# The last pair's sums and stores started earlier, and two gate products moved forward, in a hybrid encoder layer on one core

## The chip, the cores and the metric

The kernel runs on one core of one Trainium2 chip. Its time is the device time of one execution in microseconds (us). Three executions of the kernel before took 1149.3, 1150.73 and 1148.74 us; their median is 1149.3 us.

## The reference, cut to what matters

The layer is applied to two sequences of 512 tokens (prompt and sample) with the same weights, all in fp32, width 1024, feed-forward width 2816. Only the feed-forward part is touched:

```python
up = _dwconv3(_rmsnorm(x, norm2) @ w_up, conv_w, conv_b)     # (512, 5632), three taps along the tokens
gate, val = up[..., :D_FF], up[..., D_FF:]
x = x + (jax.nn.silu(gate) * val) @ w_down                   # (512, 2816) @ (2816, 1024)
g = jax.nn.sigmoid(_rmsnorm(x, norm3) @ w_ple_gate + b_ple_gate)
x = x + (p @ w_ple_proj) * g
```

## The kernel before, in words

Every matrix product is done in two parts: an operand is split into a high part (rounded, written by ScalarE) and a low part (the difference, written by VectorE), and TensorE adds three products, high by high, low by high, high by low (`mm3`, L297 to L299). So each tile that TensorE reads must have passed ScalarE first and VectorE second. The semaphores `w_hi`, `g_hi`, `uw_hi` count the high parts, `w_lo`, `g_lo`, `uw_lo` the low parts.

**The up projection** runs over 22 feature tiles, taken as 11 pairs (NPAIR = 11, `last` = 10), each pair in two blocks f = 0 and f = 1. A block is seven products over sums and differences of quarters of the operands (the kinds "1", "6", "5", "2", "7", "3", "4" of `STEADY`, in that order), 12 matmuls each. Three of them share accumulator banks that VectorE combines in between: `add_u2` (L2108), `add_v` (L2114) and `add_c22` (L2121). TensorE's kind "7" waits for `add_v`, kind "4" for `add_c22`. VectorE also splits the weights (`up_lo`, L2032), adds the outer taps (L2131, L2139) and multiplies silu(gate) by val (`product`, L2146; it counts `g_ready`). ScalarE does the centre tap, silu and the high parts. GpSimd forms the weight sums (`combine`, L2514). Pair 0 has an own entry part; pair 1 is the first one in steady order, and its VectorE block (1, 0) also holds the two products that are left over from pair 0's second block (`behind`).

**For the down projection** the kernel needs, of each pair, sums of the gated values (four tiles S, `sum_s`, L2553) and of `w_down` (four tiles T, `sum_t`, L2558). GpSimd makes both in SBUF (SB and TB, in XT) and SyncE's DMA queue stores them to HBM (`store_s` L516, `store_t` L526). They are laid down in HBM since all pairs are read back later: the down projection is 77 units n = 0 to 76, seven passes p over the 11 pairs k, and each unit needs one 256 KB weight tile (`load_down`, L579) and one 256 KB tile of activations (`load_g`, L586 or L588). There are four buffers for each; ScalarE splits (L1575, L1583), VectorE splits (L2229, L2233), TensorE does 12 matmuls. Pass 0 reads neither S nor T. Pass 1 (from unit 11) reads T tile 3 and S tile 1 of each pair, its last unit, 21, those of the last pair. When the sums are stored, their place in XT takes the residual back from HBM (`load_x2`, L537).

**What sets the order.** Each engine runs its own list in the order written, and blocks on the semaphore waits in front of an instruction. SyncE's list is one queue: a wait in it holds up every transfer behind it. `load_down(n)` waits for `w_lo` of unit n - 4, `load_g(n)` for `g_lo` of unit n - 4. GpSimd's list for the last pair is s_late and t_sums of pair 9, then a wait `g_lo >= 8` (L2620, low parts of units 0 to 7), then `s_early`, `s_pair`, `s_late` and `t_sums` of pair 10: eight operations in 128x512 fp32. `s_early` needs `g_ready` 42, `s_pair` needs 44, which is the last product of the up projection.

Of the kernel before, what the change touches and what calls it, by code (L numbers as in the profile page):

```python
# [38 lines left out]
NPAIR = FT // 2  # L39
# [47 lines left out]
def encoder(nc, x, p_in, w, y, consts):  # L87
    with ExitStack() as ctx:
# [3 lines left out]
        def sem(name):  # L92
            return ctx.enter_context(nc.semaphore(name))
# [61 lines left out]
        def quarter(f, r):  # L155

            return RAW[f][:, r // 2, 4 * (r % 2):4 * (r % 2) + 4, :]

        def s1_buf(f):
            return (RB[:, :], R[:, 1, :])[f].rearrange("p (k m) -> p k m", k=4)  # L160
# [23 lines left out]
        def up_w(v, k):  # L184

            return v[:, 1 - k // 2, 4 * (k % 2):4 * (k % 2) + 4, :]
# [44 lines left out]
        s_sum, s_out, t_in, t_sum, t_out = (sem(n) for n in ("s_sum", "s_out", "t_in", "t_sum", "t_out"))  # L231
# [33 lines left out]
        g_hi, g_lo, dn_tile, dn_ready, dn_free = (sem(n) for n in ("g_hi", "g_lo", "dn_tile", "dn_ready", "dn_free"))  # L265
# [132 lines left out]
        def _(sp):  # L398
# [108 lines left out]
            def store_g(i, f):  # L507
                sp.wait_ge(g_ready, i * 4 + (2 * f + 2))
                if f:
                    sp.dma_start(g_dram[:, 1:3, bass.ds(i * S, S)], SG[:, 1]).then_inc(g_out[1], 16)  # L510
                else:
                    sp.dma_start(g_dram[:, 0, bass.ds(i * S, S)], SG[:, 0, 1]).then_inc(g_out[0], 16)

            def store_s(i):
                sp.wait_ge(s_sum, i * 4 + 4)
                sp.dma_start(s_dram[:, bass.ds(i * 4 * S, 4 * S)], XT[:, 0:4 * S]).then_inc(s_out, 16)  # L516
# [7 lines left out]
            def store_t(i):  # L524
                sp.wait_ge(t_sum, i * 4 + 4)
                sp.dma_start(t_dram[:, bass.ds(i * 4 * S, 4 * S)], TB).then_inc(t_out, 16)  # L526
# [9 lines left out]
            def load_x2(q):  # L536
                sp.dma_start(XT[:, q * 2048:(q + 1) * 2048], xt_dram[:, q * 2048:(q + 1) * 2048]).then_inc(xt_back[q], 16)  # L537
# [32 lines left out]
            def load_down(n):  # L570
                p, k = divmod(n, NPAIR)
                if n >= 4:
                    sp.wait_ge(w_lo, T_DN + n - 3)
                if DN_W[p] is None:
                    tile = t_dram[:, (4 * k + DN_T[p]) * S:(4 * k + DN_T[p] + 1) * S]
                else:
                    f, h = DN_W[p]
                    tile = w["w_down"][(2 * k + f) * P:(2 * k + f + 1) * P, h * S:(h + 1) * S]
                sp.dma_start(up_w(WR, d_slot(n)), tile.rearrange("p (a m) -> p a m", m=P)).then_inc(wd_in[n % 4], 16)  # L579

            def load_g(n):
                p, k = divmod(n, NPAIR)
                if n >= 4:
                    sp.wait_ge(g_lo, n - 3)
                if DN_G[p] is None:
                    sp.dma_start(AR[:, n % 4, :], s_dram[:, (4 * k + DN_S[p]) * S:(4 * k + DN_S[p] + 1) * S]).then_inc(g_in[n % 4], 16)  # L586
                else:
                    sp.dma_start(AR[:, n % 4, :], g_dram[:, DN_G[p], k * S:(k + 1) * S]).then_inc(g_in[n % 4], 16)  # L588

            last = NPAIR - 1  # L590
# [11 lines left out]
            for n in range(4, NU):  # L602
                if n == last:
                    sp.wait_ge(g_out[0], 16 * NPAIR)
                if n == NPAIR:
                    sp.wait_ge(t_out, 16 * last)
                    sp.wait_ge(s_out, 16 * last)
                if n == 16:
                    sp.wait_ge(t_out, 16 * NPAIR)
                    load_x2(1)  # L610
                if n == 17:
                    sp.wait_ge(s_out, 16 * NPAIR)
                    load_x2(0)
                if n == 2 * NPAIR:
                    sp.wait_ge(g_out[1], 16 * NPAIR)
                load_down(n)
                load_g(n)
                if n == 4:
                    store_g(last, 1)
                if n == 12:  # L620
                    store_s(last)
                if n == 14:
                    store_t(last)
                if n == 8:
                    sp.wait_ge(conv_done, 4 * FT)
                    sp.wait_ge(pt_out, 16)
                    sp.dma_start(SF[:, 2048:4096], pt_dram).then_inc(p_in_sem, 16)

            def store(s):
                for t in range(TT):  # L630
                    g = s * TT + t
                    sp.wait_ge(f_out, 2 * (g + 1))
                    sp.dma_start(y[s][t * P:(t + 1) * P, :], OT[:, g % 3, :]).then_inc(out_done[g % 3], 16)
# [1063 lines left out]
        def _(dve):  # L1697
            def f32(v):
                return v.bitcast(F32)
# [329 lines left out]
            def up_lo(raw, k_slot, count):  # L2029

                dve.wait_ge(uw_hi, count)
                dve.tensor_tensor(up_w(WL, k_slot), raw, f32(up_w(WH, k_slot)), ALU.subtract).then_inc(uw_lo, 1)  # L2032
# [71 lines left out]
            def add_u2(i, f, steady=True):  # L2104

                dve.wait_ge(m_done, done_at("6", i, f, steady))
                dve.wait_ge(m_copied, copy_at(0, i, f, steady))
                dve.tensor_tensor(ps[4 * f + 1][:, :], ps[4 * f + 1][:, :], E1[:, f, :], ALU.add).then_inc(m_summed, 1 if steady else 2)  # L2108

            def add_v(i, f, steady=True):  # L2110

                dve.wait_ge(m_copied, copy_at(1, i, f, steady))
                dve.wait_ge(m_summed, sum_at(0, i, f, steady))
                dve.tensor_tensor(ps[4 * f + 2][:, :], ps[4 * f + 1][:, :], M5C[:, f, :], ALU.add).then_inc(m_summed, 1 if steady else 2)  # L2114

            def add_c22(i, f, steady=True):

                dve.wait_ge(m_done, done_at("7", i, f, steady))
                if steady:
                    dve.wait_ge(conv_done, i * 8 + (4 * f - 6))  # L2120
                dve.tensor_tensor(ps[4 * f + 3][:, :], ps[4 * f + 1][:, :], M5C[:, f, :], ALU.add).then_inc(m_summed, 1 if steady else 2)  # L2121
# [20 lines left out]
            def product(i, f, s):  # L2142

                dve.wait_ge(silu_done, i * 4 + (2 * f + s + 1))
                dve.wait_ge(conv_done, i * 8 + (4 * f + (4, 2)[s]))
                dve.tensor_tensor(SG[:, f, s, :], SG[:, f, s, :], CV[:, s, :], ALU.mult).then_inc(g_ready, 1)  # L2146
# [38 lines left out]
            def up_block(i, f, more=True, behind=False):  # L2185

                base = 7 * f
                up_lo(quarter(f, 2), UP_SLOT["7"], i * 14 + (base + 5))
                add_u2(i, f)
                if not behind:  # L2190
                    up_lo(quarter(f, 1), UP_SLOT["3"], i * 14 + (base + 6))
                add_v(i, f)
                if behind:
                    up_lo(quarter(f, 1), UP_SLOT["3"], i * 14 + (base + 6))
                up_lo(quarter(f, 3), UP_SLOT["4"], i * 14 + (base + 7))
                if more:
                    up_lo(quarter(1 - f, 1), UP_SLOT["2"], i * 14 + (base + 8))
                add_c22(i, f)
                if behind:
                    product(0, 1, 1)  # L2200
                    product(0, 1, 0)
                tap_left(i, f, 0)
                if more:
                    up_lo(quarter(1 - f, 0), UP_SLOT["1"], i * 14 + (base + 9))
                tap_right(i, f, 0)
                tap_left(i, f, 1)
                if more:
                    up_lo(S2, UP_SLOT["6"], i * 14 + (base + 10))
                tap_right(i, f, 1)
                tap_left(i, f, 2)  # L2210
                if more:
                    up_lo(s1_buf(1 - f), UP_SLOT["5"], i * 14 + (base + 11))
                tap_right(i, f, 2)
                tap_left(i, f, 3)
                product(i, f, 1)
                tap_right(i, f, 3)
                product(i, f, 0)
# [6 lines left out]
            last = NPAIR - 1  # L2224
# [158 lines left out]
        def _(pool):  # L2383
# [88 lines left out]
            for i in range(HEADS // 2):  # L2472
                last = i == HEADS // 2 - 1
# [87 lines left out]
            def s_early(i):  # L2561

                pool.wait_ge(s_out, i * 16)
                pool.wait_ge(g_ready, i * 4 + 2)
                sum_s(SB[:, 2, :], SG[:, 0, 1, :], SG[:, 0, 0, :], ALU.subtract, i * 4 + 1)
# [51 lines left out]
            up_sums(NPAIR - 1, 1)  # L2617
            s_late(NPAIR - 2)
            t_sums(NPAIR - 2)
            pool.wait_ge(g_lo, 8)  # L2620
            s_early(NPAIR - 1)
            s_pair(NPAIR - 1)
            s_late(NPAIR - 1)
# [60 lines left out]
```

## Time and profile before

| | |
|---|---|
| profiled execution, time | 1149.3 us |
| its span (first to last instruction) | 1147.5 us |
| median of three runs | 1149.3 us |
| TensorE busy | 1116.6 us, 97% |
| VectorE busy | 820.4 us, 71% |
| ScalarE busy | 559.3 us, 49% |
| GpSimd busy | 464.8 us, 41% |
| DMA, mean over the span | 141 GB/s |

The table is read with the engines in mind: TensorE is hardly ever idle, so only idle time of TensorE, and what ends it, can change the time. The profiled execution's time lies 1.8 us above its span, and equals the median, so a change of the span is read as the same change of the median.

### The profile page before, as it was taken

What the parts mean: (1) busy time and instruction counts of PE and PEld (TensorE: products, weight loads), DVE (VectorE), ACT (ScalarE), POOL (GpSimd) and SP (SyncE); (2) the same over time, 40 slices, a digit from 0 to 9 for tenths busy, and PEclk for the clock granted to TensorE, in tenths of its full rate; (3) what the DMA queues carried; (4) which work ended last, traced back from release to release, by engine and by line L of the source; (5) the groups of instructions that cost most, each with busy time, mean ns of one, the idle gap of its engine ahead of it and who ended that gap; (6) DMA issues with size and microseconds to landing.
All of it is one profiled execution on the core that took longest, in us unless ns stands there. A gap on an engine that the chain in (4) does not pass through costs nothing.

```text
span 1147.5 us, 15785 instructions
## 1 busy us (share of the span) xinstructions
PE 1116.6 (97%) x5120; PEld 894.5 (78%) x5120; DVE 820.4 (71%) x1164; ACT 559.3 (49%) x992; POOL 464.8 (41%) x405
## 2 busy tenths in 40 slices
PE   7999999999999989999999999999999999999996
PEld 6788766665888867888888888888888888888885
DVE  6594876773458799878787878787876757757565
ACT  6412577775223454445454545454564546544332
POOL 0176542322567046856585558556210202201000
PEclk9999999999999999999999999999999999999999
DMA  6611000104653116443644364435896565534341
GB/s 208 215 32 44 1 12 12 38 6 148 214 202 120 55 41 223 158 162 121 210 144 157 119 210 153 149 128 182 334 340 207 187 201 191 174 105 121 92 142 74
DMA packets 138432, 161.61 MB, mean 141 GB/s; under 512 B 8755, under 2 KB 105354, under 8 KB 133770
## 3 DMA queue, kind: packets, MB, share of 16 engines
q1 hardware_dynamic: 138080, 160.82, 41.9%
q8 instruction: 29, 0.48, 0.2%
q14 instruction: 25, 0.20, 0.1%
q10 hardware_dynamic: 298, 0.11, 0.0%
HBM read 115.55 MB, written 45.35 MB: 140 GB/s over the span
## 4 chain that ended last, share of the span: by engine, by line
PE 85%; DVE 9%; ACT 2%; issue 2%; POOL 1%; ACTq 0%; DVEq 0%; POOLq 0%
PE ps L297 26%; PE ps L299 26%; PE ps L298 26%; PE ps L859 2%; PE ps L840 2%; DVE WL L2032 1%; PE ps L710 1%; ACT SF L1173 1%; PE ps L851 1%; DVE SF L2131 1%; DVE SF L2139 1%; DVE WDHL L1889 1%; DVE col L1900 1%; PE ps L671 0%; DVE R L1882 0%
## 5 line engine op out<-in xcount | busy, mean ns | idle before, releaser
L297 PE MATMUL ps<-XH,WH 128*128 128x512 f32 x722 | 287.9, 399 | 2.0 <-DVE WL L2032 0.8
L299 PE MATMUL ps<-XH,WL 128*128 128x512 f32 x722 | 281.5, 390 | 0.0
L298 PE MATMUL ps<-XL,WH 128*128 128x512 f32 x722 | 281.4, 390 | 0.0
L297 PEld LDWEIGHTS ps<-XH,WH 128*128 128x128 f32 x722 | 135.9, 188 | 34.4 <-issue 5.4
L298 PEld LDWEIGHTS ps<-XL,WH 128*128 128x128 f32 x722 | 135.9, 188 | 29.2 <-issue 2.2
L299 PEld LDWEIGHTS ps<-XH,WL 128*128 128x128 f32 x722 | 135.7, 188 | 28.5
L297 PE MATMUL ps<-GHL,WH 128*128 128x512 f32 x394 | 153.5, 390 | 1.4 <-DVE WL L2032 1.4
L298 PE MATMUL ps<-GHL,WH 128*128 128x512 f32 x394 | 153.3, 389 | 0.0
L299 PE MATMUL ps<-GHL,WL 128*128 128x512 f32 x394 | 153.3, 389 | 0.0
L333 ACT ACTIVATE WH<-WR 128x1024 fp32r<-128x1024 f32 (+3 forms) x45 | 45.5, 1011 | 137.8 <-PE ps L299 124.1
L1466 ACT ACTIVATE SF<-ps,col 128x512 f32<-128x512 f32 x88 | 68.3, 779 | 74.5 <-PE ps L299 65.5
L2229 DVE TENSOR_TENSOR WL<-WR,WH 128x512 fp32r<-128x512 f32 x77 | 58.2, 756 | 59.8 <-ACT WH L1575 59.8
L1575 ACT ACTIVATE WH<-WR 128x512 fp32r<-128x512 f32 x77 | 48.6, 632 | 93.0 <-PE ps L299 74.0
L2633 POOL TENSOR_TENSOR SF<-SF 128x512 f32<-128x512 f32 x16 | 24.1, 1504 | 168.0 <-ACT SF L1618 168.0
L297 PEld LDWEIGHTS ps<-GHL,WH 128*128 128x128 f32 x394 | 74.0, 188 | 17.4 <-issue 2.1
L299 PEld LDWEIGHTS ps<-GHL,WL 128*128 128x128 f32 x394 | 74.0, 188 | 15.3
L298 PEld LDWEIGHTS ps<-GHL,WH 128*128 128x128 f32 x394 | 74.0, 188 | 15.3
L338 DVE TENSOR_TENSOR WL<-WR,WH 128x1024 fp32r<-128x1024 f32 (+3 forms) x45 | 61.5, 1366 | 24.7 <-ACT WH L333 24.2
L2558 POOL TENSOR_TENSOR XT<-XT 128x512 f32<-128x512 f32 x44 | 68.8, 1563 | 11.8 <-DMA XT<-in_w_down 7.7
L2139 DVE SCALAR_TENSOR_TENSOR SF<-ps,col,SF 128x511 f32<-128x511 f32 x88 | 65.2, 741 | 0.4
L2131 DVE SCALAR_TENSOR_TENSOR SF<-ps,col,SF 128x511 f32<-128x511 f32 x88 | 64.8, 737 | 0.0
L2032 DVE TENSOR_TENSOR WL<-TL,WH 128x512 fp32r<-128x512 f32 x54 | 50.4, 933 | 18.6 <-ACT WH L1422 18.6
(237 smaller groups left out, 2245.6 us busy)
## 6 DMA issues: line engine op xcount, KB each, us to landing
TL<-in_w_up SPq DMA_DIRECT2D x48, 256.0 KB, 3.6
s_scratch<-XT SPq DMA_DIRECT2D x11, 1024.0 KB, 4.7
XT<-in_w_down SPq DMA_DIRECT2D x11, 1024.0 KB, 6.5
t_scratch<-XT SPq DMA_DIRECT2D x11, 1024.0 KB, 3.8
WR<-t_scratch SPq DMA_DIRECT2D x44, 256.0 KB, 2.7
TL<-s_scratch SPq DMA_DIRECT2D x44, 256.0 KB, 2.9
WR<-in_w_up SPq DMA_DIRECT2D x40, 256.0 KB, 3.3
WR<-in_w_down SPq DMA_DIRECT2D x33, 256.0 KB, 4.1
```

What stands on the lines that cost most here:

```text
L297: pe.matmul(out, wh, xh, start=first, stop=False, skip_group_check=skip)
L298: pe.matmul(out, wh, xl, start=False, stop=False, skip_group_check=skip)
L299: return pe.matmul(out, wl, xh, start=False, stop=last, skip_group_check=skip)
L333: act.activation(WH[:, slot(n), base:cols, :], WR[:, slot(n), base:cols, :], ACT.Copy).then_inc(w_hi, 1)
L338: dve.tensor_tensor(WL[:, slot(n), base:cols, :], WR[:, slot(n), base:cols, :], WH[:, slot(n), base:cols, :].bitcast(F32), ALU.subtract).t ...
L1466: act.activation(out, ps[4 * f + bank][:, :], ACT.Identity, scale=taps_of(1, val, f), bias=taps_of(3, val, f)).then_inc(tap1, 1)
L1575: act.activation(up_w(WH, d_slot(n)), up_w(WR, d_slot(n)), ACT.Copy).then_inc(w_hi, 1)
L2032: dve.tensor_tensor(up_w(WL, k_slot), raw, f32(up_w(WH, k_slot)), ALU.subtract).then_inc(uw_lo, 1)
L2131: dve.scalar_tensor_tensor(out[:, 1:S], ps[4 * f + bank][:, 0:S - 1], taps_of(0, val, f), out[:, 1:S], ALU.mult, ALU.add).then_inc(tap0, 1)
L2139: dve.scalar_tensor_tensor(out[:, 0:S - 1], ps[4 * f + bank][:, 1:S], taps_of(2, val, f), out[:, 0:S - 1], ALU.mult, ALU.add).then_inc(con ...
L2229: dve.tensor_tensor(up_w(WL, d_slot(n)), up_w(WR, d_slot(n)), f32(up_w(WH, d_slot(n))), ALU.subtract).then_inc(w_lo, 1)
L2558: pool.tensor_tensor(out, a, b, ALU.subtract).then_inc(t_sum, 1)
```

## The change

1. VectorE, block (1, 0): the two products left over from pair 0 come before the low parts of kind "4"'s and the next block's weights, no longer behind `add_c22`.
2. GpSimd: the wait `g_lo >= 8` before the last pair's `s_early` goes.
3. SyncE: the last pair's S store goes behind the loads of unit 6 (before: unit 12), its T store behind unit 9 (before: 14). Before the loads of unit 11 the queue waits until both stores have landed (before: those of pair 9). The two loads of the residual are issued behind the loads of units 11 and 14, with no wait of their own (before: ahead of units 16 and 17, after waits for the two stores).

```diff
                 if n == NPAIR:
-                    sp.wait_ge(t_out, 16 * last)
-                    sp.wait_ge(s_out, 16 * last)
-                if n == 16:
                     sp.wait_ge(t_out, 16 * NPAIR)
-                    load_x2(1)
-                if n == 17:
                     sp.wait_ge(s_out, 16 * NPAIR)
-                    load_x2(0)
...
                 load_down(n)
                 load_g(n)
...
-                if n == 12:
+                if n == 6:
                     store_s(last)
-                if n == 14:
+                if n == 9:
                     store_t(last)
...
+                if n in (NPAIR, NPAIR + 3):
+                    load_x2(1 if n == NPAIR else 0)
...
                 if behind:
                     up_lo(quarter(f, 1), UP_SLOT["3"], i * 14 + (base + 6))
+                    product(0, 1, 1)
+                    product(0, 1, 0)
                 up_lo(quarter(f, 3), UP_SLOT["4"], i * 14 + (base + 7))
                 if more:
                     up_lo(quarter(1 - f, 1), UP_SLOT["2"], i * 14 + (base + 8))
                 add_c22(i, f)
-                if behind:
-                    product(0, 1, 1)
-                    product(0, 1, 0)
...
             t_sums(NPAIR - 2)
-            pool.wait_ge(g_lo, 8)
             s_early(NPAIR - 1)
```

VectorE in block (1, 0), before: from `add_v` (out ps2) over the two weight parts of kinds "3" and "4" (WR), that of the next block (TL), `add_c22` (out ps3) and the two products to the first tap.

```order
L2114 TENSOR_TENSOR ps2<-ps1,SF 128x512 [waits m_summed,m_copied]
L2032 TENSOR_TENSOR WL<-WR,WH 128x512 [waits uw_hi] x2
L2032 TENSOR_TENSOR WL<-TL,WH 128x512 [waits uw_hi]
L2121 TENSOR_TENSOR ps3<-ps1,SF 128x512 [waits conv_done,m_done]
L2146 TENSOR_TENSOR SF<-SF 128x512 [waits conv_done,silu_done] x2
L2131 SCALAR_TENSOR_TENSOR SF<-ps0,col,SF 128x511 [waits tap1]
```

The same stretch of VectorE in the changed kernel, whose lines are numbered 4 lower here.

```order
L2110 TENSOR_TENSOR ps2<-ps1,SF 128x512 [waits m_summed,m_copied]
L2028 TENSOR_TENSOR WL<-WR,WH 128x512 [waits uw_hi]
L2142 TENSOR_TENSOR SF<-SF 128x512 [waits conv_done,silu_done] x2
L2028 TENSOR_TENSOR WL<-WR,WH 128x512 [waits uw_hi]
L2028 TENSOR_TENSOR WL<-TL,WH 128x512 [waits uw_hi]
L2117 TENSOR_TENSOR ps3<-ps1,SF 128x512 [waits conv_done,m_done]
L2127 SCALAR_TENSOR_TENSOR SF<-ps0,col,SF 128x511 [waits tap1]
```

The products moved ahead of two weight parts and of `add_c22`; nothing is added or removed.

SyncE before, from the loads of unit 6 to those of unit 11: no store stands between them (SF<-pt_scratch is the transfer behind unit 8).

```order
L588 DMA TL<-g_scratch 128x512 [waits g_lo]
L579 DMA WR<-in_w_down 128x512 [waits w_lo]
L588 DMA TL<-g_scratch 128x512 [waits g_lo]
L579 DMA WR<-in_w_down 128x512 [waits w_lo]
L588 DMA TL<-g_scratch 128x512 [waits g_lo]
L627 DMA SF<-pt_scratch 128x2048 [waits pt_out,conv_done]
L579 DMA WR<-in_w_down 128x512 [waits w_lo]
L588 DMA TL<-g_scratch 128x512 [waits g_lo]
L579 DMA WR<-in_w_down 128x512 [waits w_lo,g_out0]
L588 DMA TL<-g_scratch 128x512 [waits g_lo]
L579 DMA WR<-t_scratch 128x512 [waits w_lo,s_out,t_out]
```

SyncE in the changed kernel, from the S store behind unit 6 to the first residual load behind unit 11.

```order
L516 DMA s_scratch<-XT 128x2048 [waits s_sum]
L579 DMA WR<-in_w_down 128x512 [waits w_lo]
L588 DMA TL<-g_scratch 128x512 [waits g_lo]
L579 DMA WR<-in_w_down 128x512 [waits w_lo]
L588 DMA TL<-g_scratch 128x512 [waits g_lo]
L621 DMA SF<-pt_scratch 128x2048 [waits pt_out,conv_done]
L579 DMA WR<-in_w_down 128x512 [waits w_lo]
L588 DMA TL<-g_scratch 128x512 [waits g_lo]
L526 DMA t_scratch<-XT 128x2048 [waits t_sum]
L579 DMA WR<-in_w_down 128x512 [waits w_lo,g_out0]
L588 DMA TL<-g_scratch 128x512 [waits g_lo]
L579 DMA WR<-t_scratch 128x512 [waits w_lo,s_out,t_out]
```

Two 1 MB stores with a wait each now stand among the loads of units 7 to 10, and the wait ahead of unit 11 is for these stores.

## Rows read from the trace of the kernel before

**Rows 1.** Busy time from 457 to 1100 us; columns are named in the first line.
```profile
core 0: us, PE busy (x) PEld busy (x) DVE busy (x) ACT busy (x) POOL busy (x), PEclk, DMA share, GB/s
457.00:1100.00 643.00, 643.00 (x2850) 532.04 (x2849) 471.10 (x651) 311.09 (x517) 265.73 (x183) 1.00 0.52 175
```
**Rows 2.** TensorE's waits from 405 to 1100 us, all of them.
```profile
PE ps L297 <- DVE WL L2032: 4.4, 4, 2.2
PE ps L297 <- DVE ps L2114: 1.1, 2, 0.6
```
**Rows 3.** Timeline of DVE, block (1, 0): start, duration, instruction.
```profile
436.57 2.38 DVE L2032 TENSOR_TENSOR WL<-WR,WH 128x512 fp32r<-128x512 f32 x2
438.88 1.77 DVE L2032 TENSOR_TENSOR WL<-TL,WH 128x512 fp32r<-128x512 f32 x1
440.57 0.69 DVE L2121 TENSOR_TENSOR ps<-ps,SF 128x512 f32<-128x512 f32 x1
441.18 1.28 DVE L2146 TENSOR_TENSOR SF<-SF 128x512 f32<-128x512 f32 x2
...
455.88 0.68 DVE L2114 TENSOR_TENSOR ps<-ps,SF 128x512 f32<-128x512 f32 x1
```
**Rows 4.** Timeline of POOL in the same stretch.
```profile
436.64 1.77 POOL L2514 TENSOR_TENSOR R<-R,TL 128x512 f32<-128x512 f32 x1
...
442.60 1.29 POOL L2553 TENSOR_TENSOR XT<-XT,SF 128x512 f32<-128x512 f32 x1 [2.50 <-DVE SF L2146]
```
**Rows 5.** Timeline of PE: start of kind "4", then start of the next kind "7".
```profile
442.31 0.39 PE L297 MATMUL ps<-CHL,WH 128*128 128x512 f32 x1
...
456.62 0.50 PE L297 MATMUL ps<-WDHL,WH 128*128 128x512 f32 x1 [0.55 <-DVE ps L2114]
456.96 0.40 PE L298 MATMUL ps<-WDHL,WH 128*128 128x512 f32 x1
```
**Rows 6.** Timeline of DVE: last product, low parts of unit 3; then units 9 and 11.
```profile
812.92 0.69 DVE L2146 TENSOR_TENSOR SF<-SF 128x512 f32<-128x512 f32 x1
813.53 0.69 DVE L2229 TENSOR_TENSOR WL<-WR,WH 128x512 fp32r<-128x512 f32 x1
814.13 0.69 DVE L2233 TENSOR_TENSOR GHL<-TL,GHL 128x512 fp32r<-128x512 f32 x1
...
828.51 1.75 DVE L2233 TENSOR_TENSOR GHL<-TL,GHL 128x512 fp32r<-128x512 f32 x1
...
835.30 1.78 DVE L2233 TENSOR_TENSOR GHL<-TL,GHL 128x512 fp32r<-128x512 f32 x1
```
**Rows 7.** Timeline of POOL: sums of pair 9, then of the last pair.
```profile
794.65 6.19 POOL L2558 TENSOR_TENSOR XT<-XT 128x512 f32<-128x512 f32 x4 [7.72 <-DMA XT<-in_w_down]
823.11 3.36 POOL L2553 TENSOR_TENSOR XT<-SF 128x512 f32<-128x512 f32 x2 [22.26 <-DVE GHL L2233]
```
**Rows 8.** Timeline of PE: first matmuls of units 0, 6 and 17.
```profile
807.63 0.39 PE L297 MATMUL ps<-GHL,WH 128*128 128x512 f32 x1
...
823.96 0.39 PE L297 MATMUL ps<-GHL,WH 128*128 128x512 f32 x1
...
853.94 0.47 PE L297 MATMUL ps<-GHL,WH 128*128 128x512 f32 x1
```
**Rows 9.** Timeline of SyncE's queue: unit 13, the T store, the first residual load.
```profile
830.14 0.43 SPq L579 DMA_DIRECT2D WR<-t_scratch  x1
...
836.56 0.34 SPq L526 DMA_DIRECT2D t_scratch<-XT  x1
...
841.43 0.33 SPq L537 DMA_DIRECT2D XT<-xt_scratch  x1
```
**Rows 10.** Timeline of ACT: high parts of units 6 (activations) and 13 (weights).
```profile
820.33 0.63 ACT L1583 ACTIVATE GHL<-TL 128x512 fp32r<-128x512 f32 x1
...
835.33 0.63 ACT L1575 ACTIVATE WH<-WR 128x512 fp32r<-128x512 f32 x1 [0.76 <-DMA WR<-t_scratch]
```
**Rows 11.** DMA from 816 to 828 us, mean rate of all transfers.
```profile
DMA packets 2107, 4.64 MB, mean 387 GB/s; under 512 B 233, under 2 KB 233, under 8 KB 1978
```

## The prediction

> **What bounds the kernel now.** I read the busy shares first: TensorE is busy 1116.6 of 1147.5 us. Next the busy time by stretch: from 457 to 1100 us TensorE's busy time fills the whole 643.00 us [rows 1]. Then its waits: from 405 to 1100 us there are six in all, 5.5 us, all on VectorE [rows 2], and all of them before 457. The down projection, where the larger part of the change lies, has nothing to give back; it can only lose, by a wait that is new there. So I asked how much lead VectorE and the DMAs have over TensorE, and what the earlier GpSimd work does to it. For that I read the timelines of the two places side by side.
>
> **How GpSimd costs VectorE time.** A low part takes VectorE 0.69 us alone (unit 3 [rows 6]). While GpSimd runs sums, the same instructions last 1.75 to 1.78 us, and from 828.51 to 835.30 four starts lie (835.30 - 828.51) / 4 = 1.70 us apart [rows 6], against 0.60 us (813.53 to 814.13). In that stretch GpSimd's sums follow each other at the same step. The two engines take turns, each waiting until the other's operation is over, and one GpSimd operation costs VectorE 1.10 us. Operations of VectorE that read an accumulator bank keep their time (`add_c22`, 0.69 us [rows 3]).
>
> **Part 1, the two products in block (1, 0).** Before, behind `add_v`: two weight parts, 436.57 to 438.95, with a GpSimd operation (436.64 [rows 4]) between them; the third from 438.88 to 440.65, also held up by GpSimd; `add_c22` at 440.57, the products at 441.18, alone: 1.28 us for both [rows 3]. TensorE starts kind "4" at 442.31 with no wait [rows 5], 1.05 us after `add_c22` is done (441.26).
> Now: the products take the second and third place, so they are what the same two GpSimd operations hold up, and end at 440.65. They release GpSimd's `s_pair_copied`, which came 0.14 us after the products before (442.46 to 442.60 [rows 3, 4]), so it is ready at 440.79. VectorE's second weight part starts at 440.57 and goes first, GpSimd is next, and the third weight part, issued at 441.17, takes the long form, 1.77 us, to 442.94. `add_c22` starts at 442.86 and ends at 443.55, TensorE's kind "4" at 443.60 (0.05 us of passing on: `add_v` ends at 456.56, kind "7" starts at 456.62 [rows 3, 5]). That is a new wait of 443.60 - 442.31 = 1.29 us. A start after a wait costs 0.11 us more, as 456.62 to 456.96 is 0.34 us where the usual step is 0.23 [rows 5]. New loss: 1.40 us.
> What goes in return: kind "7" would start at 442.31 + 5 x 2.72 = 455.91 and started at 456.62 [rows 5], a loss of 0.71 + 0.11 = 0.82 us. In the new order TensorE gets there at 457.31, and VectorE's chain, with the same work, at about 456.5, so this wait goes. Net: 1.40 - 0.82 = +0.58 us. Bounds: -0.8 (the old wait goes and the new one doesn't come, if GpSimd's sums don't get between) and +1.4.
>
> **Part 2, the removed wait on GpSimd.** Pair 9's sums end at 794.65 + 6.19 = 800.84 [rows 7]; `s_early` can follow at once, in a time when VectorE has little to do. `s_pair` needs the last product, done at 812.92 + 0.69 = 813.61 [rows 6]. So seven operations (two, one, four) start about 813.75 in place of 823 to 836. The load for the T sums stands in SyncE's queue where it stood, ahead of unit 4's tiles, so it is no obstacle. VectorE then has units 3 to 6 to split. The low weight part of unit 3 is already running (813.53), and from 814.13 on each of the next seven low parts takes a turn with one GpSimd operation:
> activations of unit 3 from 814.13 to 815.91; of unit 4 from 817.53 to 819.31; of unit 5 from 820.93 to 822.71; of unit 6 from 824.33 to 826.11 (step 2 x 1.70, duration 1.78).
> TensorE's units start at 807.63 + 2.72 n (unit 6: 823.96 [rows 8]), so they would start at 815.79, 818.51, 821.23 and 823.96. Its lags are 0.17, 0.85, 1.53 and 826.16 - 823.96 = 2.20 us, with the slow start 2.31 us. The high parts are no limit (unit 6's is done at 820.96 [rows 10]). Then GpSimd is done (814.2 + 7 x 1.70 = 826), and VectorE does a unit in 1.2 us against TensorE's 2.72. Before, the same contention fell on units 8 to 11 with some 4 us of lead, and was hidden. Bounds: 0 if VectorE keeps a lead I don't see, and 7 x 1.10 - 0.97 = 6.7 us if none of it is absorbed beyond unit 3's lead (814.82 to 815.79). I take 2.3, since it is a count of turns at a pitch that rows show.
> Unit 17 started 0.06 us late, and slow, at 853.94 [rows 8], behind the residual loads; these come earlier now, so I take off 0.1 us.
>
> **Part 3, SyncE's queue.** The S store waits for `s_late`, the third operation, at about 818.9, and unit 7's loads stand behind it. The T store goes at about 825.7, and unit 11's loads wait until it has landed. The busy queue moves 387 GB/s [rows 11], 2.7 us per 1 MB; a T store with nothing ahead of it took 841.43 - 836.56 = 4.9 us [rows 9], so a transfer starts some 2.2 us after its issue. Unit 13's tile, issued at 830.14 right behind an S store, was taken up at 835.33 [rows 9, 10], 5.2 us later. So unit 7's tiles are there by 825.0, and split behind unit 6 by 827.3, against 826.67 + 2.3 = 829.0. The T store here queues behind seven transfers and lands about 832.8 instead of 830.5. Unit 11's tiles land at 836.1, are split by 837.5, and are needed at 837.55 + 2.3 = 839.9. Unit 12, behind a residual load of 1 MB, lands at 840.0, split 841.4, needed 842.6. The thinnest margin is 1.2 us, so I take 0; at 10% less rate unit 12 would lose some 0.5 us. The bounds are 0 and 4 us (worked out with the rivals).
> The page on DMA in the Trainium skill ("DMA: Bandwidth & Descriptors", section Bandwidth) puts the limit of traffic between HBM and SBUF at about 358 GB/s per core, below the 387 that this trace shows for 12 us. By an estimate from that page each megabyte takes 2.9 us, unit 12's tiles come about 1.4 us later, and the sum would be higher by about 0.3 us; the trace's rate is used.
>
> **The sum.** 0.58 + 2.31 - 0.1 + 0 = +2.8 us, on the profiled execution's span 1147.5 and on its time 1149.3, which is the median: 1152.1 us. Nothing behind takes it back, since TensorE has no other wait until 1100 us [rows 1].
>
> **The rivals.**
> *The contention is absorbed.* GpSimd's turns fall where VectorE would idle, as they did for units 8 to 11. Part 1 alone is left: 1149.9 us. For it: two low parts alone take 1.2 us of a unit's 2.72, so VectorE has slack on average. Against it: with turns they take 3.4 us, and the lead of 0.97 us at unit 3 is smaller than one turn of 1.70. Chance 0.18.
> *SyncE's stops decide.* The wait for the T store ahead of unit 11 and 4.5 MB of early transfers leave the tiles of units 10 to 12 late. At 310 GB/s (1 MB in 3.4 us) unit 10's tiles are ready at 839.5, needed at 837.1, and unit 12 adds 1.8: +4.1 more, 1156.2 us. It decides once the T store lands behind about 835. For it: the DMAs are saturated there. Against it: the rate of rows 11. Chance 0.14.
> *Not slower: VectorE's block (1, 0) really gets shorter.* The products go early enough that GpSimd's first sum of S is behind the third weight part; `add_c22` is then at 441.8, kind "4" waits for nothing and the 0.82 us at 456 go, and in the down projection the turns leave VectorE the precedence. The time would be 1149.3 - 0.8 = 1148.5 us. It decides if GpSimd needs over 0.4 us from the products to its sum; the row says 0.14. Chance 0.08.
> *The change does nothing in its larger part*, if GpSimd's sums were held by something else until 823. The only wait of theirs that fell so late is that on VectorE's low part of activations [rows 7], so I give this nothing of its own.
>
> **Chances and range.** Forecast 0.60, with its own range 1151.2 to 1153.6; absorbed 0.18; stops 0.14; shorter 0.08. Two tenths of a per cent, 2.3 us, is about what a measurement of this kernel can tell from no change. Of the forecast's own case I put 0.46 above +2.3 us and 0.14 below. Slower: 0.46 + 0.14 = 0.60. Faster by that much isn't reachable by any mechanism here: 0.03 for the unseen. Same: 0.37. The range for 8 in 10 is 1149.5 to 1155.5 us: it takes in the absorbed case and half way to the stops.
>
> **What would show it.** Part 1: a wait of TensorE of some 1.3 us on `add_c22` about 442, and none on `add_v` about 456. Part 2: GpSimd's seven sums from 813.7 to about 826, low parts of 1.7 us there, and four waits of TensorE on the low parts of units 3 to 6, growing to 2.2 us in total. Part 3: no wait of TensorE on DMA-fed parts of units 7 to 12. I am wrong if the low parts stay at 0.69 us beside GpSimd's sums, if units 3 to 6 start on time, or if units 10 to 12 start late.

## The result, and the profile after

The changed kernel takes 1158.3 us (median of four, 1157.69 to 1158.83) against 1150.0 us in the same runs: a ratio of 1.0067, 95% interval 1.0052 to 1.0082, so +6 to +9 us. The forecast was +2.8 us, with 1155.5 as the upper end. It is slower, as forecast, but by about 8 us. Of ten executions of the changed kernel on record nine took 1156.8 to 1158.9 us and one 1154.5.

The profiled execution took 1158.92 us, its span is 1157.1 (before: 1149.3 and 1147.5), so 9.6 us are to be found. TensorE's waits, all of them from 400 to 1100 us, are the first view (engine, tile and line, what it waited for: us, times, longest). To them belong the two rows of before [rows 2].

```profile
PE ps L297 <- DVE GHL L2228: 5.0, 5, 3.5
PE ps L297 <- DVE WL L2028: 4.4, 4, 2.1
PE ps L297 <- DVE ps L2117: 1.2, 1, 1.2
PE ps L297 <- DVE ps L2110: 0.5, 1, 0.5
```

Where these waits are shows in TensorE's timeline: kind "4" of block (1, 0), then units 4, 5, 6, 10 and 12, each with the wait in brackets.

```profile
444.58 0.50 PE L297 MATMUL ps<-CHL,WH 128*128 128x512 f32 x1 [1.17 <-DVE ps L2117]
...
821.01 0.47 PE L297 MATMUL ps<-GHL,WH 128*128 128x512 f32 x1 [0.42 <-DVE GHL L2228]
824.41 0.47 PE L297 MATMUL ps<-GHL,WH 128*128 128x512 f32 x1 [0.43 <-DVE GHL L2228]
827.79 0.47 PE L297 MATMUL ps<-GHL,WH 128*128 128x512 f32 x1 [0.40 <-DVE GHL L2228]
...
839.14 0.47 PE L297 MATMUL ps<-GHL,WH 128*128 128x512 f32 x1 [0.22 <-DVE GHL L2228]
848.38 0.47 PE L297 MATMUL ps<-GHL,WH 128*128 128x512 f32 x1 [3.55 <-DVE GHL L2228]
```

A wait in brackets is about 0.17 us less than the start moved by, since a matmul is drawn 0.39 us long and the next one starts 0.23 us after it. So I account by starts:

| stretch | how it is read | us |
|---|---|---|
| to `add_v` of block (1, 0), before anything changed | 436.93 - 435.97 | +0.96 |
| to unit 0 | 809.20 - 807.63, less the 0.96 | +0.61 |
| units 0 to 6 | 827.79 - 809.20 = 18.59, before 16.33 [rows 8] | +2.26 |
| units 6 to 12 | 848.38 - 840.27 = 8.11 late, less 3.83 | +4.28 |
| unit 12 to the last unit | 1027.1 - 848.38 = 178.72, before 1017.5 - 840.27 = 177.23 | +1.49 |

The sum is 9.60 us; the tail adds nothing. The first entry lies ahead of every changed instruction, so it is not the change's; that it is there is one reason why this pair of profiles shows more than the medians do.

VectorE and GpSimd in block (1, 0) (compare [rows 3, 4]; everything is 0.96 us later here):

```profile
437.54 0.68 DVE L2028 TENSOR_TENSOR WL<-WR,WH 128x512 fp32r<-128x512 f32 x1
438.13 3.48 DVE L2142 TENSOR_TENSOR SF<-SF 128x512 f32<-128x512 f32 x2
441.54 0.68 DVE L2028 TENSOR_TENSOR WL<-WR,WH 128x512 fp32r<-128x512 f32 x1
442.14 1.78 DVE L2028 TENSOR_TENSOR WL<-TL,WH 128x512 fp32r<-128x512 f32 x1
443.85 0.68 DVE L2117 TENSOR_TENSOR ps<-ps,SF 128x512 f32<-128x512 f32 x1
```

```profile
441.76 1.61 POOL L2548 TENSOR_TENSOR XT<-XT,SF 128x512 f32<-128x512 f32 x1 [0.69 <-DVE SF L2142]
```

The two products last 3.48 us instead of 1.28, the third weight part is held up by GpSimd's sum, and `add_c22` stands at 443.85.

The same two engines in the down projection (compare [rows 6, 7]): low parts of units 3, 4 and 6, and GpSimd's first and last sums.

```profile
815.69 1.79 DVE L2228 TENSOR_TENSOR GHL<-TL,GHL 128x512 fp32r<-128x512 f32 x1
817.40 1.77 DVE L2224 TENSOR_TENSOR WL<-WR,WH 128x512 fp32r<-128x512 f32 x1
...
825.88 1.77 DVE L2228 TENSOR_TENSOR GHL<-TL,GHL 128x512 fp32r<-128x512 f32 x1
```

```profile
815.32 1.61 POOL L2548 TENSOR_TENSOR XT<-SF 128x512 f32<-128x512 f32 x1 [11.52 <-DVE SF L2142]
...
820.39 6.71 POOL L2553 TENSOR_TENSOR XT<-XT 128x512 f32<-128x512 f32 x4
```

Seven sums, seven long low parts. Up to here it is as predicted. What wasn't is in SyncE's queue: the S store, the T store, unit 11's weights behind the wait, the residual load, unit 12's activations (compare [rows 9]). Below them stands ScalarE taking up unit 11's activations, then unit 12's weights and activations.

```profile
820.34 0.34 SPq L516 DMA_DIRECT2D s_scratch<-XT  x1
...
827.13 0.34 SPq L526 DMA_DIRECT2D t_scratch<-XT  x1
...
836.39 0.33 SPq L579 DMA_DIRECT2D WR<-t_scratch  x1
...
837.24 0.43 SPq L537 DMA_DIRECT2D XT<-xt_scratch  x1
...
838.20 0.42 SPq L586 DMA_DIRECT2D TL<-s_scratch  x1
```

```profile
839.75 0.63 ACT L1579 ACTIVATE GHL<-TL 128x512 fp32r<-128x512 f32 x1
845.62 0.63 ACT L1571 ACTIVATE WH<-WR 128x512 fp32r<-128x512 f32 x1 [5.24 <-DMA WR<-t_scratch]
846.88 0.63 ACT L1579 ACTIVATE GHL<-TL 128x512 fp32r<-128x512 f32 x1 [0.63 <-DMA TL<-s_scratch]
```

The queue stands still from 828.45 to 836.39 us. Unit 11's tiles, the first behind the stop, are there 3.4 us after it ends (839.75). Unit 12's activations, issued at 838.20, are there only 8.7 us later. Between the two is the residual's megabyte, issued at 837.24 and landed 7.7 us later, at 844.9 (last figure of the line, from issue to landing):

```profile
XT<-xt_scratch SPq DMA_DIRECT2D x1, 1024.0 KB, 7.7
```

So it landed 5.2 us after unit 11's tiles, and unit 12's tiles landed behind it. The busy time by stretch shows DMA and clock (last three columns: granted clock, DMA share, GB/s):

```profile
836.00:838.00 2.00, 2.00 (x10) 1.65 (x10) 0.30 (x1) 0.97 (x2) 0.00 (x0) 1.00 0.34 77
838.00:840.00 2.00, 1.78 (x9) 1.18 (x8) 1.27 (x3) 1.16 (x3) 0.00 (x0) 1.00 0.86 300
...
849.50:853.50 4.00, 4.00 (x13) 3.10 (x12) 3.55 (x6) 4.00 (x10) 0.00 (x0) 0.57 0.98 371
853.50:856.00 2.50, 2.50 (x13) 2.05 (x12) 1.84 (x4) 2.40 (x6) 0.00 (x0) 1.00 0.79 262
```

The DMAs nearly run dry (77 GB/s) before unit 11's and 12's tiles and the 1 MB come at once. And TensorE's granted clock falls behind the wait: 0.57 over 4 us, 13 matmuls where 17.6 fit at a step of 0.227 us. So time was lost here while TensorE was busy, which the statement ahead of the prediction, that only idle time of TensorE can change the time, leaves out.

### The profile page after: what moved, and what is told of

Same layout as the page of the kernel before. It is cut to its first block, busy times and chain, and to the rows that moved or that the text cites. A ratio compares the mean times of both kernels' runs of the same rounds, so it can differ in the third digit from the quotient of the medians.

```text
span 1157.1 us, 15784 instructions
## 1 busy us (share of the span) xinstructions
PE 1120.7 (97%) x5120; PEld 896.1 (77%) x5120; DVE 822.5 (71%) x1164; ACT 558.3 (48%) x992; POOL 465.3 (40%) x405
## 4 chain that ended last, share of the span: by engine, by line
PE 83%; DVE 8%; DMA 2%; issue 2%; ACT 2%; POOL 2%; SPq 0%; DVEq 0%; POOLq 0%; ACTq 0%
PE ps L297 25%; PE ps L299 25%; PE ps L298 25%; PE ps L855 2%; PE ps L836 2%; DVE WL L2028 1%; DMA t_scratch<-XT 1%; PE ps L706 1%; DMA TL<-s_scratch 1%; ACT SF L1169 1%; PE ps L847 1%; DVE SF L2127 1%; DMA SF<-in_x_prompt 1%; DVE WDHL L1885 1%; PE ps L667 1%
```

## The experiments

Ratios are against the kernel before, run beside each kernel; the us behind them are differences of medians, by the intervals good to about 1 us each way. A table of all profiles stands at the end of this section. Theory A is that three separate costs add up: turns in block (1, 0), turns at units 3 to 6, and SyncE's stop together with the residual load ahead of unit 12.

**e1, the products alone.** The change's part 1 on the kernel before.

```diff
                 if behind:
                     up_lo(quarter(f, 1), UP_SLOT["3"], i * 14 + (base + 6))
+                    product(0, 1, 1)
+                    product(0, 1, 0)
...
                 add_c22(i, f)
-                if behind:
-                    product(0, 1, 1)
-                    product(0, 1, 0)
```

> The kernel before with the two products moved alone. Theory A (what was predicted, and what the profile after seems to show): a wait of TensorE of about 1.2 us on add_c22 at kind 4 of block (1, 0), none on add_v at the next kind 7, +0.6 us in all (1150.6 against 1150.0), no other wait behind. Theory B (the whole loss is SyncE's queue in the down projection and the products cost nothing): +0.0 us, no wait on add_c22.

Measured: 1151.4 against 1150.7 us, ratio 1.0008 (0.9999 to 1.0017), +0.7 us. In the trace the wait is on `add_c22`, that on the next `add_v` is gone:

```profile
PE ps L297 <- DVE ps L2121: 1.2, 1, 1.2
PE ps L297 <- DVE GHL L2232: 0.6, 1, 0.6
PE ps L297 <- DVE ps L2114: 0.5, 1, 0.5
PE ps L297 <- issue: 0.4, 1, 0.4
```

A's mechanism is confirmed; its +0.6 us lies within the interval, but so does zero. Not expected: waits at unit 17 (0.58) and unit 11 (0.35), where nothing was changed.

**e2, GpSimd's wait alone removed**, on the kernel before.

```diff
             t_sums(NPAIR - 2)
-            pool.wait_ge(g_lo, 8)
             s_early(NPAIR - 1)
```

> The kernel before with GpSimd's wait removed alone; SyncE's queue as before. Theory A: GpSimd's seven sums from about 813.7 to 826 us, VectorE's low parts there 1.7 to 1.8 us each, TensorE late at units 4, 5 and 6 (about 0.4 us each, growing to 2.3 us), none at unit 10 or 12, granted clock 1.00 throughout: +2.3 us. Theory B (the waits of units 4 to 6 come from late tiles, and go with the old queue): units 3 to 6 on time, +0.0 us.

Measured: 1151.5 us, ratio 1.0007 (0.9997 to 1.0016), +0.8 us. The trace has the waits of 0.42, 0.43 and 0.40 us at units 4, 5, 6 (821.02, 824.42, 827.82) with the old queue, so they don't come from late tiles: B falls. But A's total of +2.3 us, a ratio of 1.0020, lies outside the interval, and zero inside; the profiles of e9 and the table below say why.

**e3, the changed kernel with the old SyncE queue.** Stores, waits and residual loads are back at their old places.

```diff
-                if n == 6:
+                if n == 12:
                     store_s(last)
-                if n == 9:
+                if n == 14:
                     store_t(last)
...
-                if n in (NPAIR, NPAIR + 3):
-                    load_x2(1 if n == NPAIR else 0)
```

> The changed kernel with SyncE's queue as it was before: both other parts stay. Theory A: the sum of the two, +2.9 us; the waits of units 10 and 12 (0.2 and 3.6 us) and the fall of the granted clock behind unit 12 are gone, so 5.4 us less than the changed kernel. Theory B: as the kernel before, +0.0 us. Theory C (GpSimd's earlier sums also make the loads late, whatever the queue's order): a wait at unit 10 to 12 stays, +5 us or more.

Measured: 1153.3 us, ratio 1.0016 (1.0005 to 1.0027), +2.6 us. No wait at units 10 and 12, clock 1.00 from 846 to 856 us. So the queue's new order is worth about 1158.3 - 1153.3 = 5 us (different runs; 5.8 by the profiles), as A said, and C falls.

**e5, the stores early, the waits for them and the residual loads late.** On the changed kernel:

```diff
                 if n == NPAIR:
+                    sp.wait_ge(t_out, 16 * last)
+                    sp.wait_ge(s_out, 16 * last)
+                if n == 16:
                     sp.wait_ge(t_out, 16 * NPAIR)
+                    load_x2(1)
+                if n == 17:
                     sp.wait_ge(s_out, 16 * NPAIR)
+                    load_x2(0)
...
-                if n in (NPAIR, NPAIR + 3):
-                    load_x2(1 if n == NPAIR else 0)
```

> The changed kernel, with the stores at their new places (behind units 6 and 9), but the waits for them and the residual loads back where they were before (ahead of units 16 and 17). Theory A (unit 12 is late because the queue stands still until the T store has landed and a 1 MB residual load is ahead of its tiles): no wait at unit 12, the 0.2 us at unit 10 stays, +3.3 us against the kernel before. Theory D (the early stores alone, by their 2 MB among the loads of units 7 to 10, make units 10 to 12 late): the wait at unit 12 stays over 1 us, +5 us or more.

Measured: 1153.8 us, ratio 1.0025 (1.0014 to 1.0037), +3.1 us; only the three waits at units 4 to 6 in the down projection. The 2 MB of early stores by themselves cost no wait that the profile lists, not even the one at unit 10. D falls.

**e4, the stop stays, the residual loads late.** On the changed kernel:

```diff
+                if n == 16:
+                    load_x2(1)
+                if n == 17:
+                    load_x2(0)
...
-                if n in (NPAIR, NPAIR + 3):
-                    load_x2(1 if n == NPAIR else 0)
```

> The changed kernel with the wait for both stores still ahead of unit 11's loads, but the two residual loads back ahead of units 16 and 17. Theory A (unit 12 needs both: the stopped queue and the 1 MB ahead of its tiles): unit 11 as in the changed kernel, unit 12's tiles issued at about 837.3 us land by 842, no wait there or under 0.3 us, granted clock 1.00, +3.3 us against the kernel before, as with no hold. Theory E (the stop alone makes the queue late): a wait of 2 us or more at unit 12 stays, +5 us or more.

Measured: 1152.9 against 1151.5 us, ratio 1.0013 (1.0003 to 1.0022), +1.4 us. The stop is as long as in the changed kernel (T store issued at 824.30, unit 11's loads at 834.03), yet unit 12 is on time; unit 10 waits 0.63 us (the second line):

```profile
824.97 0.47 PE L297 MATMUL ps<-GHL,WH 128*128 128x512 f32 x1 [0.40 <-DVE GHL L2230]
...
836.78 0.47 PE L297 MATMUL ps<-GHL,WH 128*128 128x512 f32 x1 [0.63 <-DVE GHL L2230]
```

E falls. The smaller total than e5's is not a gain: this profile has the same waits as e5's and the one at unit 10 besides, and takes 0.8 us more from block (1, 0) on (table). The stop alone leaves unit 12 on time; the residual loads can't be had early without the stop, since they overwrite what the stores read, so that half wasn't tried alone.

**e6, the first residual load one unit later**, behind unit 12's loads.

```diff
-                if n in (NPAIR, NPAIR + 3):
-                    load_x2(1 if n == NPAIR else 0)
+                if n in (NPAIR + 1, NPAIR + 3):
+                    load_x2(1 if n == NPAIR + 1 else 0)
```

> The changed kernel with the first residual load one unit later, behind the loads of unit 12, the second behind unit 14 as before it. Theory A: unit 12 on time, unit 13 behind the 1 MB and late in its place, by 1 to 2 us since one unit more of lead was won; the granted clock falls behind it only if that wait is long enough, so this shows a wait between 0.4 us (clock kept in the units 4 to 6) and 3.55 us (clock lost). +4 to +6 us against the kernel before. Theory F (the residual load is slow in itself wherever it stands): a wait of 3.5 us as in the changed kernel, moved to unit 13.

Measured: 1154.7 us, ratio 1.0028 (1.0019 to 1.0037), +3.2 us. Unit 12 is on time, unit 13 waits, but 0.34 us, less than the 1 to 2 expected:

```profile
847.34 0.47 PE L297 MATMUL ps<-GHL,WH 128*128 128x512 f32 x1 [0.34 <-DVE GHL L2228]
```

The clock stays at 1.00 behind it. One place in the queue turns 3.55 us of waiting into 0.34, so F falls. Two things changed at once: unit 13 is needed 2.72 us after unit 12, and the megabyte itself came faster, 6.7 us from issue to landing where the changed kernel's took 7.7:

```profile
XT<-xt_scratch SPq DMA_DIRECT2D x1, 1024.0 KB, 6.7
```

**e7, memsets in place of the seven sums**, on the kernel before, with the old queue. This kernel leaves out seven of the last pair's eight sums. Its one execution took 1147.3 us.

```diff
-            pool.wait_ge(g_lo, 8)
             s_early(NPAIR - 1)
-            s_pair(NPAIR - 1)
-            s_late(NPAIR - 1)
-            t_sums(NPAIR - 1)
...
+            for j, q in enumerate((0, 1, 3)):
+                pool.memset(SB[:, q, :], 0.0).then_inc(s_sum, 1)
...
+            for j, q in enumerate((0, 1, 3, 2)):
+                pool.memset(TB[:, q, :], 0.0).then_inc(t_sum, 1)
```

> The kernel before without GpSimd's wait, and with the last pair's seven sums after s_early replaced by writes of zeros to the same tiles (this leaves out the last pair's sums). Theory A (two operations that read SBUF take turns): VectorE's low parts of units 3 to 6 at 0.69 us although GpSimd works at the same time, units 4 to 6 on time. Theory G (any GpSimd work or its semaphores there slow VectorE): low parts over 1 us and waits at units 4 to 6 as with the sums, though shorter.

The low parts beside GpSimd's memsets keep their 0.69 us, and no unit waits:

```profile
812.34 0.69 DVE L2233 TENSOR_TENSOR GHL<-TL,GHL 128x512 fp32r<-128x512 f32 x1
813.74 0.69 DVE L2229 TENSOR_TENSOR WL<-WR,WH 128x512 fp32r<-128x512 f32 x1 [0.71 <-ACT WH L1575]
814.37 0.69 DVE L2233 TENSOR_TENSOR GHL<-TL,GHL 128x512 fp32r<-128x512 f32 x1
```

```profile
811.95 1.70 POOL L2624 MEMSET XT<- 128x512 f32 x3 [11.53 <-DVE SF L2146]
813.70 2.28 POOL L2628 MEMSET XT<- 128x512 f32 x4
```

So it is not that GpSimd works, writes or signals there, but that its sums also read SBUF: G falls. The Trainium skill ("SBUF — State Buffer", section Who interferes with whom) says that a VectorE instruction with two SBUF inputs contends with a GpSimd one that reads SBUF, not with one that only writes. The trace agrees on both sides: 1.7 us per turn beside sums, 0.69 us beside memsets.

**e9 and e10, both kernels again.**

> The kernel before once more, for a second profile. Theory A: block (1, 0) and (1, 1) as before (waits of 0.5 us each on add_v), and waits of 0.3 to 0.6 us at unit 11 or 17 in this execution or not, since the leads there were 0.5 and 0 us in the first profile. Theory H: all units on time.

> The changed kernel once more, for a second profile. Theory A: waits of about 0.4 us at units 4, 5 and 6 and of 3 to 4 us at unit 12, with the granted clock down behind it. Theory I (the wait at unit 12 was an accident of one execution): under 1 us there.

The kernel before, in its second profile (1150.87 us), waits at units 11 and 17:

```profile
838.67 0.47 PE L297 MATMUL ps<-GHL,WH 128*128 128x512 f32 x1 [0.36 <-issue]
855.54 0.47 PE L297 MATMUL ps<-GHL,WH 128*128 128x512 f32 x1 [0.26 <-DVE GHL L2233]
```

H falls. Unit 11 starts 0.9 us late here (838.67 against 807.85 + 11 x 2.72 = 837.77), at the end of the sums' turns. The first profile (1149.3 us, the second fastest of four) happened to have only a trace of the second wait. Neither is in the profiles of e2, e3 and e5, where GpSimd's sums are early and TensorE runs 2.4 us later: e2 pays 2.4 us, and gets back 1.4 against an execution like this one. The changed kernel repeats itself: 0.39, 0.40, 0.40, then 0.35 at unit 10 and 3.43 at unit 12 (1159.21 us), and clock 0.58 from 849.5 to 853.5. I falls.

**e8, a version from the findings**, on the kernel before: three leads are widened.

```diff
-            pool.wait_ge(g_lo, 8)
             s_early(NPAIR - 1)
+            pool.wait_ge(g_lo, 8)
...
-                if n == 17:
+                if n == 20:
                     sp.wait_ge(s_out, 16 * NPAIR)
                     load_x2(0)
```

In block (1, 1), `add_v` also goes ahead of the low part of kind "3".

> A version made from the findings, on the kernel before: GpSimd's wait stands behind s_early, so that one of eight sums leaves the contended stretch; the second residual load goes ahead of unit 20 in place of 17; in block (1, 1) add_v comes before the low part of kind 3. Theory A: the wait on add_v at about 457 shrinks from 0.55 to about 0.1 us, no waits at units 11 and 17, which the kernel before shows in some executions (0.35 and 0.58 us in the run with the products alone): -0.6 us where those waits don't occur and -1.7 us where they do, so 1149 to 1150 against 1150.7. Theory H (these leads don't matter): +0.0 us.

Measured: 1149.0 against 1151.5 us, ratio 0.9977 (0.9966 to 0.9988), -2.6 us: faster than both kernels, by more than expected. The wait on `add_v` at 455 us fell to 0.18, and no unit waits. The profile accounts for 0.5 us against the first profile of the kernel before and 1.9 against the second (table); the rest of the 2.6 it doesn't show.

**e11 and e12, two of its three parts alone**: the hunk at `n == 17` of e8's diff, and the hunk at `g_lo`.

> Of the combined version only its second residual load: the kernel before, with it ahead of unit 20 instead of 17. Theory A (unit 17's tiles are late because two 1 MB loads stand ahead of them): no wait at unit 17, the 0.4 us at unit 11 may stay; -0.3 to -0.7 us. Theory J (the wait goes to unit 20 with the load): a wait there, +0.0 us.

> Of the combined version only the place of GpSimd's wait: the kernel before, with the wait behind s_early, so that seven sums and not eight fall among the units 8 to 11. Theory A (unit 11's 0.4 us wait is the end of that contention): no wait at unit 11; unit 17 may still be late by 0.1 to 0.7 us; -0.5 us. Theory K (unit 11's wait has nothing to do with the sums): it stays, +0.0 us.

The residual load at 20: 1150.2 us, ratio 1.0001 (0.9993 to 1.001), nothing measurable; its profile has no wait at unit 17 or 20, but the first profile of the kernel before has none that is listed either. GpSimd's wait moved: 1149.0 against 1150.6, ratio 0.9989 (0.9979 to 0.9998), -1.3 us. Unit 11's low part of activations, the last of its contended stretch in e9 and free in e12:

```profile
836.78 1.79 DVE L2233 TENSOR_TENSOR GHL<-TL,GHL 128x512 fp32r<-128x512 f32 x1
```

```profile
836.46 0.68 DVE L2233 TENSOR_TENSOR GHL<-TL,GHL 128x512 fp32r<-128x512 f32 x1
```

One turn less where the lead was 0.5 us, and unit 11 is on time. This and the ratio speak against K, but one profile doesn't exclude it, since unit 11 was on time in the first profile of the kernel before too. Between A and J the measurement doesn't decide (A's -0.3 us lies inside). The two don't add up to e8's 2.6 us; its third part, `add_v` first, shows about 0.4 us in the trace, and what is left stays open.

**All profiles side by side.** The start of kind "7" in block (1, 0), behind its wait on `add_v`, is the last point ahead of the first changed instruction. It lies at 434.80 to 438.30 us in the fourteen profiles, so executions differ by up to 3.5 us before the change can have done anything, which is more than most of the effects here. From that start to the end of the span the profiles can be compared (us):

| profile | span | start of kind "7" | from there to the end |
|---|---|---|---|
| before | 1147.5 | 436.72 | 710.8 |
| before again (e9) | 1149.1 | 436.90 | 712.2 |
| e7, memsets | 1145.5 | 434.91 | 710.6 |
| e8, the version from the findings | 1146.2 | 435.90 | 710.3 |
| e11, residual load at 20 | 1147.9 | 436.86 | 711.0 |
| e12, GpSimd's wait moved | 1147.6 | 436.70 | 710.9 |
| e1, products alone | 1151.2 | 438.26 | 712.9 |
| e2, sums early alone | 1151.3 | 438.30 | 713.0 |
| e3, both, old queue | 1151.8 | 438.22 | 713.6 |
| e5, early stores, late residual | 1152.0 | 438.22 | 713.8 |
| e4, stop, late residual | 1149.4 | 434.80 | 714.6 |
| e6, residual one unit later | 1151.8 | 437.38 | 714.4 |
| after | 1157.1 | 437.68 | 719.4 |
| after again (e10) | 1157.4 | 437.89 | 719.5 |

Against 710.8 the products and the early sums together cost 2.8 us (e3), the early stores 0.2 more (e5), the stop another 0.8 (e4), and the residual load right behind unit 11 another 4.8, of which 1.5 are the clock: 8.6 in all. Against the second profile of the kernel before it is 1.4 less, 7.2 us; the measured 8 lies between. Most of e1's 2.1 us are waits at units 11 and 17, as in e9. Part of the difference ahead of kind "7" is the clock as well (last section).

## Why the prediction was wrong, step by step

**Part 1 held.** Predicted: a wait on `add_c22` moving kind "4" by 1.29 us, no wait on `add_v` behind, +0.58 net. Found: `add_c22` moved as worked out, +0.61 by starts; e1's +0.7 us agrees, with an interval that reaches zero.

**Part 2 held as a mechanism and in the profiled pair.** Predicted lags of units 3 to 6: 0.17, 0.85, 1.53, 2.20. Found against 809.20 + 2.72 n: 0.26 (817.62), 0.93, 1.61, 2.27. e2 shows it alone, e7 its cause. What it missed is on the side of before: I read one execution, and took the thin leads at units 11 and 17 as held, when other executions lose there. I took 0.1 us off for unit 17; e9 loses 1.4 us more there than the first profile. So the net of part 2 is +2.2 against the one (713.0 - 710.8) and +0.8 against the other (713.0 - 712.2).

**Part 3 failed, and with it the sum.** The prediction took 0 for SyncE's queue and had the mechanism only as a rival, with chance 0.14. Three steps of it failed.

(1) The T store's landing, which ends the stop. It was to land 7.1 us after its issue (825.7 to 832.8) and took 9.3 (827.13 to 836.39), 2.2 us more. The rate is the smaller part of this. The 387 GB/s of [rows 11] come from a stretch with only the end of one 512 KB store in it, but e5, with both early stores in it, moves as much from 820 to 836 us (first line; the changed kernel 361, second line):

```profile
DMA packets 2081, 6.16 MB, mean 385 GB/s; under 512 B 233, under 2 KB 233, under 8 KB 1696
DMA packets 1874, 5.77 MB, mean 361 GB/s; under 512 B 217, under 2 KB 217, under 8 KB 1489
```

What was priced too short is the queue ahead of the store, with another megabyte (SF<-pt_scratch) in it. From its issue to its landing, 827.13 to 836.37, the DMAs moved:

```profile
DMA packets 922, 3.23 MB, mean 349 GB/s; under 512 B 111, under 2 KB 111, under 8 KB 667
```

At 387 GB/s these 3.23 MB would take 8.3 us (estimate), so 0.9 of the 2.2 us are the rate. The same store takes 9.0 us in e5, without any stop.

(2) The residual's megabyte. Unit 11's activations came 3.4 us after the stop's end, as forecast (3.3), so the restart itself cost nothing beyond it. Unit 12's were to come 3.9 us behind them, 2.7 of it for the megabyte. They came 7.1 us behind them (839.75 to 846.88), and the megabyte alone took 5.2. In e4, with the same stop and no residual load, they came 2.2 us behind. Steps (1) and (2), 2.2 and 3.3 us, use up the 1.2 us of margin and leave 4.3. The prediction named 10% less rate as worth 0.5 us, and 4 us as the bound of all of part 3.

(3) The clock, 1.5 us, was in no term.

The limit of 358 GB/s, from the page that the prediction names (the Trainium skill, "DMA: Bandwidth & Descriptors", section Bandwidth), would not have helped: by the prediction's own estimate from it the sum would still have been 5 us short, and e5's 385 GB/s over 16 us lie above it.

The rival on SyncE's stops was right in place (units 10 to 12) and in size (+4.1 against +4.3), but for its weight and for the balance between units: it had most of the loss at unit 10 (2.3 us), which lost 0.4. So the agreement of the two sums is chance. With the same stop and no residual load, e4 loses 0.63 us at unit 10 and nothing at unit 12: most of the price is paid by the tile that queues behind another megabyte. The forecast's direction was right, and for its own reasons: parts 1 and 2, as e3 shows, cost the 2.8 us that the sum gave.

What isn't settled: why that megabyte was slow. The transfers of the queue landed in the order of their issue, and it landed 5.2 us after the tile ahead of it (839.7 to 844.9; 5.7 in e10), while the same load took 3.1 us behind its predecessor one unit later (e6, 841.3 to 844.4) and in the kernel before (843.3 to 846.4). The rates in these stretches, 317, 358 and 387 GB/s, explain a part; in its 5.2 us 1.65 MB moved, so some of it was of the tiles behind. No run had the early residual load without the stop. Nor is it settled how e8's gain divides.

## What to carry to other kernels

Where an engine is busy without a gap, moving work earlier cannot gain there; ask of each moved item which lead it eats, and place it where the lead is largest: the same seven sums cost nothing at units 8 to 11 in one execution and about 1 us in another, but 2.4 us at units 3 to 6. A wait put in a DMA queue costs twice: while it holds, and again when a large transfer is then issued ahead of a small tile that is needed soon. Read thin leads (under 0.5 us) as waits of other executions. Size a transfer's landing by adding up all that is queued ahead of it. And where effects are of the size of the spread between executions, compare profiles from the last point ahead of the change.

## What the runs showed of the hardware

- VectorE operations with two inputs in SBUF (the low parts, the products) and GpSimd's sums took turns, at 1.70 us per pair, in every kernel where both had work waiting; a turn costs VectorE 1.1 us. GpSimd's memsets cost it nothing (e7).
- TensorE's granted clock fell from its upper level, 2.4 GHz, to 1.2 GHz (0.50 from 850 to 853 us) 1.3 us after the wait of 3.55 us at unit 12 ended, and was back after seven matmuls that were 0.63 us long where 0.39 is usual; the loss was 1.5 us (e10: the same behind 3.43 us). The waits of 0.2 to 0.6 us in the down projection never had this behind them.
- A wait of 2.1 to 2.2 us that ends at 417 to 421 us, which all fourteen profiles have and the change doesn't touch, was followed by the lower clock in six of them (e2, e4, e5, e6, e7, e8) and not in the other eight, both kernels among these. So the length of the wait alone doesn't tell, and executions of one kernel can differ by it. The kernel before (granted clock 1.00) and e2 (0.60), where the same wait ends 1.6 us later:

```profile
419.00:423.00 4.00, 3.26 (x13) 2.40 (x14) 4.00 (x6) 2.02 (x4) 2.45 (x2) 1.00 0.23 66
420.00:424.00 4.00, 3.23 (x8) 2.55 (x9) 4.00 (x6) 2.61 (x5) 1.86 (x2) 0.60 0.22 66
```
